# A depthwise convolution of two chunks moved from one diagonal stationary matrix and a vector chain to sixteen 32x32 tiles of the array

## The reference, cut to what matters

```python
def conformer_conv(h, w_pw1, b_pw1, w_dw, b_dw, ln_g, ln_b, w_pw2, b_pw2):
    u = h @ w_pw1 + b_pw1
    a, gate = jnp.split(u, 2, axis=-1)
    u = a * jax.nn.sigmoid(gate)
    u = lax.conv_general_dilated(u, w_dw[:, None, :], window_strides=(1,),
        padding=[(15, 15)], ..., feature_group_count=D_MODEL) + b_dw
    u = jax.nn.silu(layer_norm(u, ln_g, ln_b))
    return u @ w_pw2 + b_pw2
```

## Time and profile before

| | us |
|---|---|
| median of three runs | 2699.52 |
| the profiled execution | 2699.71 |
| its span | 2697.9 |
| TensorE busy | 2617.3 (97%) |
| VectorE busy | 1937.0 (72%) |
| ScalarE busy | 1224.2 (45%) |
| granted TensorE clock, mean | 0.98 |

### The profile page before, as it was taken

One profiled execution on the slowest core, in us unless ns is written; L12 is line 12 of the kernel. 1 busy time (PEld: TensorE's weight loads), 2 busy tenths in 40 slices (PEclk: granted clock), 3 DMA queues, 4 the chain that ended last, 5 costly groups with the idle time before them and its releaser, 6 DMA issues.

```text
span 2697.9 us, 39482 instructions
## 1 busy us (share of the span) xinstructions
PE 2617.3 (97%) x14741; PEld 2283.7 (85%) x14741; DVE 1937.0 (72%) x2749; ACT 1224.2 (45%) x1595; POOL 101.7 (4%) x145
## 2 busy tenths in 40 slices
PE   5799999999998999999999999998999999999998
PEld 4788888888887888888888888887888888888887
DVE  6987778886888888855666657998676644566554
ACT  2245644444554655544555552004454443444443
POOL 0011111100001000000000000000000000000000
PEclk7699999999999999999999999999999999999999
DMA  9898677765777777755666554552666555666554
GB/s 361 306 299 258 214 249 241 246 202 161 230 255 237 234 246 248 239 186 188 189 190 188 187 164 145 152 154 83 204 181 190 187 188 190 189 190 187 188 187 133
DMA packets 492727, 557.35 MB, mean 207 GB/s; under 512 B 18872, under 2 KB 458425, under 8 KB 492345
## 3 DMA queue, kind: packets, MB, share of 16 engines
q1 hardware_dynamic: 474169, 488.50, 56.4%
q0 software_dynamic: 18432, 67.12, 8.0%
HBM read 553.45 MB, written 2.10 MB: 206 GB/s over the span
## 4 chain that ended last, share of the span: by engine, by line
PE 91%; DVE 5%; DMA 3%; issue 1%; ACT 1%; SPq 0%; POOL 0%; DVEq 0%; ACTq 0%
PE ps L1631 53%; PE ps L1633 26%; PE ps L1961 8%; DMA att<-in_w_ada 2%; DVE wlo L949 1%; DVE tCDE L1072 1%; PE ms L1979 1%; PE ms L1682 0%; DVE att L1072 0%; PE ms L1815 0%; PE ms L1662 0%; DVE norm_rows L1053 0%; PE ms L1705 0%; DVE norm_rows L988 0%; DMA ada<-in_w_ada 0%
## 5 line engine op out<-in xcount | busy, mean ns | idle before, releaser
L949 DVE TENSOR_TENSOR wlo<-raw,whi 128x1024 fp32r<-128x1024 f32 x794 | 971.1, 1224 | 612.8 <-ACT whi L582 603.8
L1631 PE MATMUL ps<-xhl,whi 128*128 128x512 f32 x4352 | 1385.9, 400 | 15.5 <-DVE xhl L1529 6.4
L582 ACT CAST whi<-raw 128x1024 fp32r<-128x1024 f32 x794 | 831.7, 1051 | 1059.7 <-PE ps L1633 1049.2
L1633 PEld LDWEIGHTS ps<-xhl,wlo 128*128 128x128 f32 x4352 | 822.9, 189 | 195.3
L1633 PE MATMUL ps<-xhl,wlo 128*128 128x256 f32 x4352 | 859.5, 279 | 0.0
L1631 PEld LDWEIGHTS ps<-xhl,whi 128*128 128x128 f32 x4352 | 669.1, 190 | 25.6 <-issue 25.3
L1631 PE MATMUL ps<-ghl,whi 128*128 128x512 f32 x1024 | 319.5, 393 | 0.0
L1633 PEld LDWEIGHTS ps<-ghl,wlo 128*128 128x128 f32 x1024 | 192.2, 188 | 44.5
L1961 PE MATMUL ps<-xg,raw 128*128 128x256 f32 x1024 | 221.3, 379 | 0.0
L1631 PE MATMUL ps<-fhl,whi 128*128 128x512 f32 x704 | 219.3, 392 | 0.0
L1961 PEld LDWEIGHTS ps<-xg,raw 128*128 128x128 f32 x1024 | 194.5, 190 | 26.4
(11 more groups left out here) (263 smaller groups left out, 1452.2 us busy)
## 6 DMA issues: line engine op xcount, KB each, us to landing
raw<-in_w_in SPq DMA_DIRECT2D x176, 512.0 KB, 4.4
raw<-in_w_up SPq DMA_DIRECT2D x176, 512.0 KB, 3.9
ada<-in_w_ada POOLq DMA_DIRECT2D x128, 512.0 KB, 4.8
raw<-in_ffn_w_up SPq DMA_DIRECT2D x128, 512.0 KB, 3.8
raw<-in_ffn_w_down SPq DMA_DIRECT2D x128, 512.0 KB, 3.4
raw<-in_conv_w_pw SPq DMA_DIRECT2D x96, 512.0 KB, 3.7
raw<-in_w_down SPq DMA_DIRECT2D x88, 512.0 KB, 3.3
att<-in_w_ada SPq DMA_DIRECT2D x32, 1024.0 KB, 8.7
```

What stands on the lines that cost most here:

```text
L582: nc.scalar.copy(whi[t % SPL][:, :, :], raw[t % RAW][:, :, :]).then_inc(s_hi, 1)
L949: nc.vector.tensor_tensor(wlo[t % SPL][:, :, :], raw[t % RAW][:, :, :], whi[t % SPL][:, :, :].bitcast(F32), ALU.subtract).then_inc(s_lo, 1)
L1631: mm(o[:, m, :, :], whi[t % SPL][:, c, m * P:(m + 1) * P], x, start=first and c == 0, stop=last and c == KC - 1, skip_group_check=True)
L1633: ins = mm(o[:, m, 0, :], wlo[t % SPL][:, c, m * P:(m + 1) * P], x[:, 0, :], start=False, stop=last and c == KC - 1, skip_group_check=True)
```

## The change

Both chunks go to TensorE, which is used as sixteen tiles of 32x32. A tile takes 32 channels (a row strip) and writes 32 PSUM partitions (a column strip). Column strip `lane` takes taps 8*lane to 8*lane+7 (seven for the last), so that a strip of 32 channels is convolved in four partial sums, which lie on the four groups of 32 partitions of one bank; the four row strips have a bank each. A chunk is 31 taps times 4 strips, 124 matmuls with 32x32 stationary and 256 columns, in the order: tap within the lane, lane, strip. The partial sums are copied from PSUM to `lanes`, two strips by ScalarE and two by VectorE, and folded by TensorE: for each strip a 128x32 stationary matrix of four stacked identities adds the four lanes and puts them on the strip's 32 partitions. ScalarE reads the folded chunk out with the bias, and the ones matmul adds it to the mean. The stationary 32x32 diagonals of all taps are made by VectorE with one multiplication a chunk, in place of ScalarE's 31; the constants grow by 32 columns. `taps_alternating` is gone. The mean's sum moves from `bank_o` to a bank of `ps[1]`.

```diff
@@ -78,7 +78,10 @@
 G_DN2 = [169, 193]
-BY_DIAGONAL = 15
+BY_TILES = (14, 15)
+QUAD = 32
+LANES = P // QUAD
+LANE_TAPS = -(-TAPS // LANES)
 COL_KI, COL_GATE = 7168, 7248
@@ -150,7 +153,8 @@
 C_ID, C_SW128, C_SW64, C_TRI, C_PAST, C_NEG, C_FREQ, C_SIGN = 0, 128, 256, 384, 512, 896, 1280, 1282
-NCONST = 1284
+C_FOLD = 1284
+NCONST = C_FOLD + QUAD
@@ -158,6 +162,7 @@
     c[i, C_ID + i] = 1
+    c[i, C_FOLD + i % QUAD] = 1
     c[i, C_SW128 + (i + 64) % 128] = 1
@@ -257,9 +262,9 @@
         pg = sb("pg", [P, PC, T], F32, conv)
-        odd = sb("odd", [P, T], F32, conv)
+        lanes = sb("lanes", [P, 2, LANES, T], F32, conv)
         by_pairs = sb("by_pairs", [P, 2, T], F32, conv)
-        diag = sb("diag", [P, TAPS, P], F32, conv)
+        strip_diag = sb("strip_diag", [P, 2, TAPS, QUAD], F32, conv)
         conv.close()
@@ -267,6 +272,8 @@
+        lane_halves = [[ps[a][:, :, 0, :] for a in range(2)], [ms[a][:, 0:3:2, :] for a in range(2)]]
+        sum_mean = ps[1][:, 0, 0, :]
         turned_out = xg[:, 0:DC, :].rearrange("p (h c) t -> p h (c t)", h=2)
@@ -369,8 +376,11 @@
         s_edge = sem("padding_cleared")
-        s_diag = sem("tap_diagonals_made")
-        s_dwt = sem("depthwise_chunk_by_tensor")
+        s_diag = sem("strip_diagonals_made")
+        s_lanes = sem("depthwise_lanes_by_tensor")
+        s_lanesa = sem("depthwise_lanes_copied_by_scalar")
+        s_lanesv = sem("depthwise_lanes_copied_by_vector")
+        s_dwt = sem("depthwise_lanes_added")
         s_dwtc = sem("depthwise_chunk_copied")
@@ -824,9 +834,6 @@
             act.wait_ge(s_used, SPL + T_PW1)
-            for tap in range(TAPS):
-                ins = nc.scalar.activation(diag[:, tap, :], ident, ACT.Copy, scale=col("conv_w_dw_2", DC * tap + BY_DIAGONAL))
-            ins.then_inc(s_diag, 1)
             act.wait_ge(s_free[(G_PW1 + 1) % 2], free_at(G_PW1 + 1))
@@ -841,8 +848,12 @@
                 split_hi(0, T_PW2 + q)
-            act.wait_ge(s_dwt, 1)
-            nc.scalar.activation(ucv[:, BY_DIAGONAL, :], ms[0][:, 0, :], ACT.Identity, bias=col("conv_b_dw_2", BY_DIAGONAL)).then_inc(s_dwtc, 1)
+            for k in range(2):
+                act.wait_ge(s_lanes, k + 1)
+                nc.scalar.copy(lanes[:, k, 0:2, :], lane_halves[k][0]).then_inc(s_lanesa, 1)
+            for k, c in enumerate(BY_TILES):
+                act.wait_ge(s_dwt, k + 1)
+                nc.scalar.activation(ucv[:, c, :], ps[0][:, k, 0, :], ACT.Identity, bias=col("conv_b_dw_2", c)).then_inc(s_dwtc, 1)
@@ -1446,23 +1457,6 @@
-            def taps_alternating(c, before):
-
-                for tap in range(TAPS):
-                    src = upad[:, c, tap:tap + T]
-                    w = col("conv_w_dw_2", DC * tap + c)
-                    dst = odd[:, :] if tap % 2 else ucv[:, c, :]
-                    if tap == 0:
-                        dve.wait_ge(s_u, c + 1)
-                        nc.vector.tensor_scalar(dst, src, w, col("conv_b_dw_2", c), ALU.mult, ALU.add).then_inc(s_dwd, 1)
-                    elif tap == 1:
-                        nc.vector.tensor_scalar(dst, src, w, None, ALU.mult).then_inc(s_dwd, 1)
-                    else:
-                        dve.wait_ge(s_dwd, before + tap - 1)
-                        nc.vector.scalar_tensor_tensor(dst, src, w, dst, ALU.mult, ALU.add).then_inc(s_dwd, 1)
-                dve.wait_ge(s_dwd, before + TAPS)
-                nc.vector.tensor_tensor(ucv[:, c, :], ucv[:, c, :], odd[:, :], ALU.add).then_inc(s_dwd, 1)
-
@@ -1497,6 +1491,10 @@
             dve.wait_ge(s_used, SPL + T_PW1)
+            by_tap = cols[:, AT["conv_w_dw_2"]:AT["conv_w_dw_2"] + DC * TAPS].rearrange("p (t c) -> p t c", c=DC)
+            for k, c in enumerate(BY_TILES):
+                nc.vector.tensor_tensor(strip_diag[:, k, :, :], cons[:, C_FOLD:C_FOLD + QUAD].unsqueeze(1).to_broadcast([P, TAPS, QUAD]),
+                                        by_tap[:, :, c:c + 1].to_broadcast([P, TAPS, QUAD]), ALU.mult).then_inc(s_diag, 1)
             rooted(pa, G_PW1, T_PW1 + 4)
@@ -1504,10 +1502,12 @@
                 add_pair(s - 1)
-            taps_alternating(14, 7 * 2 * TAPS)
+            for k in range(2):
+                dve.wait_ge(s_lanes, k + 1)
+                nc.vector.tensor_copy(lanes[:, k, 2:4, :], lane_halves[k][1]).then_inc(s_lanesv, 1)
...
             dve.wait_ge(s_mean, 1)
-            sv.did(nc.vector.tensor_scalar(nwt[:, :], bank_o[:, 0:T], 1.0 / D, None, ALU.mult))
+            sv.did(nc.vector.tensor_scalar(nwt[:, :], sum_mean, 1.0 / D, None, ALU.mult))
             sv.wait()
@@ -1974,16 +1974,34 @@
             pe.wait_ge(s_edge, 2)
-            pe.wait_ge(s_diag, 1)
-            for tap in range(TAPS):
-                ins = mm(ms[0][:, 0, :], diag[:, tap, :], upad[:, BY_DIAGONAL, tap:tap + T], start=tap == 0, stop=tap == TAPS - 1)
-            ins.then_inc(s_dwt, 1)
+            pe.wait_ge(s_diag, 2)
+            for k, c in enumerate(BY_TILES):
+                for n in range(LANE_TAPS):
+                    for lane in range(LANES):
+                        tap = LANE_TAPS * lane + n
+                        if tap == TAPS:
+                            continue
+                        for strip in range(LANES):
+                            here = slice(QUAD * strip, QUAD * (strip + 1))
+                            ins = mm(lane_halves[k][strip // 2][QUAD * lane:QUAD * (lane + 1), strip % 2, :], strip_diag[here, k, tap, :], upad[here, c, tap:tap + T],
+                                     start=n == 0, stop=tap in (LANE_TAPS * (lane + 1) - 1, TAPS - 1), skip_group_check=True)
+                ins.then_inc(s_lanes, 1)
+            def lanes_added(k):
+
+                pe.wait_ge(s_lanesa, k + 1)
+                pe.wait_ge(s_lanesv, k + 1)
+                for strip in range(LANES):
+                    ins = mm(ps[0][QUAD * strip:QUAD * (strip + 1), k, 0, :], cons[:, C_FOLD:C_FOLD + QUAD], lanes[:, k, strip, :], start=True, stop=True)
+                ins.then_inc(s_dwt, 1)
+
+            lanes_added(0)
             pe.wait_ge(s_pair, 6)
-            pe.wait_ge(s_dwd, 15 * TAPS + 1)
-            for i, x in enumerate((by_pairs[:, 0, :], by_pairs[:, 1, :], ucv[:, 14, :], ucv[:, 15, :])):
-                if i == 3:
-                    pe.wait_ge(s_dwtc, 1)
-                ins = mm(bank_o[:, 0:T], ones[:, :], x, start=i == 0, stop=i == 3)
+            for m in range(2):
+                mm(sum_mean, ones[:, :], by_pairs[:, m, :], start=m == 0, stop=False, skip_group_check=True)
+            lanes_added(1)
+            for k, c in enumerate(BY_TILES):
+                pe.wait_ge(s_dwtc, k + 1)
+                ins = mm(sum_mean, ones[:, :], ucv[:, c, :], start=False, stop=k == 1, skip_group_check=True)
             ins.then_inc(s_mean, 1)
...
             for j in range(8):
```

## The result

| | before | after |
|---|---|---|
| median of 13 runs each, us | 2700.69 | 2705.61 |
| the profiled execution, us | 2699.71 | 2702.47 |
| its span, us | 2697.9 | 2700.6 |
| first tile or diagonal product starts, us | 1840.93 | 1842.97 |
| from there to the mean read by VectorE, us | 15.42 | 15.47 |

The ratio is 1.0018, with a 95% interval of 1.0010 to 1.0025: 4.9 us slower. The table already tells where to look. The stretch that the change rewrites takes as long as before. Most of the loss stands ahead of it: of the 2.7 us between the two profiled executions, 2.04 are a late start of the first tile, 0.05 lie in the stretch, and 0.6 lie behind it, where nothing was changed; their cause is open.

A forecast was written before the change was run, and what follows sets the result against it. The kernel was taken as a chain of matmuls, TensorE busy 97%. Tiles 13.3 + fold 1.07 + pair sums 0.86 + fold 1.07 + read-out 0.68 + ones 0.60 = 17.6 us against 15.42, 2.2 slower: 2701.7, range 2694.5 to 2719.

The forecast's parts named there:

- 16 KB more of constants at the start: nothing.: Loading the wider constants at the start of the program was claimed to cost nothing.
- Sixteen tiles, 13.3 us: Tile matmuls of both chunks on TensorE: four row strips at a time, products in order within a strip, 13.3 us.
- The port: Tile weight loads: if one goes at a time through a common port, 27 ns each, 496 take 13.4 us.
- rival A: Faster: column strips overlap as well, tiles take 6.9 us, total 2695.3, or 2694.0 with folds all at once; chance 0.19.
- rival B: Slower: instruction supply limits the tiles at 58 ns a load and matmul, 28.8 us, total 2717.2; chance 0.22.
- The folds: TensorE's adding of a chunk's lanes behind the tiles: 1.07 us each, 0.43 all at once, 1.72 in series.
- The pair sums: TensorE adds the two pair sums for the mean after the first fold: 0.86 us.
- read-out and ones: After chunk 15's fold: matmul end and ScalarE's read-out 0.68 us, then the ones matmul 0.60 us.
- The hidden parts: Small diagonals (2.4 us) and lane copies were claimed hidden beside other work; nothing was given for dropping ScalarE's 31 diagonals.
- C: Slower: lanes of one strip don't overlap, tiles 26.7 us and folds 1.72 each, total 2716.4; chance 0.14.
- D: The change doesn't do what it says: tiles run in series, 106.6 us, total near 2796; chance 0.04.
- first case: Tile phase with all sixteen tiles running at once: 3.4 us a chunk, 6.9 us for both.

The follow-up runs named there:

- e1: The changed kernel with constants as narrow as before, VectorE adding up the fold matrix from four identity blocks: 2700.88 us, ratio 1.0000.
- e2: The kernel before with only its constants 32 columns wider: 2704.86 us, ratio 1.0017.
- e5: The kernel before with the constants' tile 32 columns wider in SBUF alone, nothing more loaded: 2704.12 us, ratio 1.0013.
- e0: The changed kernel measured once more, unaltered: 2704.91 us, ratio 1.0019.
- e3: The changed kernel with 128 instead of 256 columns in all tile products but the first of each lane: 2704.14 us in one execution.
- e10: e7 with the landing tiles also begun at multiples of 512 bytes: 2696.51 us, ratio 0.9989.
- e11: e10 a second time: 2697.80 us, ratio 0.9989.
- e7: e1 with chunk 14 shared, TensorE making taps 0 to 11 and VectorE taps 12 to 30: 2699.63 us, ratio 0.9997.
- e12: e7 a second time: 2699.40 us, ratio 0.9994.

## Why the prediction came near by the wrong sum

The range (2694.5 to 2719) held, and the forecast that the change loses a little came true. The number, 2701.7, was 3.9 us low, and the forecast's own range of 2698 to 2705 was missed by 0.6. The reason failed. Forecast was +2.2 us, all from the stretch; found is 4.9 us, with +0.05 in the stretch and e1, e2 and e5 show 3 to 5 us of it to come from the start of the program. One error of 2.1 us upward in the stretch stood against one of 3 to 5 us downward at the start, so that the sum came near is luck. By its own steps:

- **"16 KB more of constants at the start: nothing."** This is the step that failed. It was right on the bytes (the wider load landed in 4.5 us where 4.2 were) and didn't ask what lies behind the constants in SBUF. Their 128 bytes a partition moved the landing tile of the first modulation off a multiple of 512 bytes. The loads there are waited for, the rate fell from 402 to 381 GB/s, and five waits grew by 3.6 us. e1 takes this away and has 4.7 us less than after (2700.88 against 2705.61, and 4.0 less than e0); e5 puts it alone into the kernel before, 3.1 us.
- **Sixteen tiles, 13.3 us: 11.9 measured.** The mechanism was wrong with the size. Forecast were row strips side by side with the lanes in order, and weight loads in turns; the records show sixteen tiles at once and thirty loads within 0.1 us. The port was no limit: the stream's 19.4 ns a pair (14.3 in e3) is under its 27. The column strips overlap, which was rival A's case, but A's 6.9 us aren't reached: a stream at hand takes 19.4 ns a matmul, 9.6 us for 496, where A's columns would be 13.9 ns each. The rest of the 11.9 us is the two pauses, where the starts stand 0.89 and 1.12 us apart, and the last matmul's own time. The pauses fit rival B's mechanism, the supply of instructions, though at 27 to 32 ns a pair over the second half and not 58 over all. (B's bound is a little off too: 32 ns a pair would lose 4.6 us, and the 5.4 us of 0.2% begin at 33 ns.)
- **The folds, 1.07 us each: 0.57.** They ran nearly all at once (the forecast's lower end was 0.43). **The pair sums**, 0.86 forecast, 1.11; **read-out and ones**, 1.28 forecast, 1.33. So 13.3 + 1.07 + 0.86 + 1.07 + 1.28 = 17.6 stands against 11.9 + 0.57 + 1.11 + 0.57 + 1.33 = 15.5.
- **The hidden parts**, the small diagonals, the copies and ScalarE's 31 diagonals, were hidden. The granted clock stayed at 1.00 in the tiles, and the first piece of the next product moved with the mean, by 2.08 and 2.09 us.
- **Rival A** would have decided below 11.1 us of tiles; measured 11.9. **C** and **D** are out by the records of the first 0.1 us.

The Trainium skill, "TensorE: Matmul & The Clock Gate", Part 3, says that a pack of sixteen such tiles runs 10.6 times as fast as in series, each starting some 4 ns after the last. In the trace the sixteen matmuls of the first pack do start within 0.11 us, but some 7.5 ns apart, not 4. In this stream of 31 packs each matmul takes 19.4 ns while instructions are at hand, where the series needs 215: 11 times, near the page's factor. Over all 496, with the pauses, it is 11.9 us where 106.6 would be the series, 9.0 times. The prediction took this rule for the 6.9 us of its first case. By the page's factor it is 106.6 / 10.6 = 10.1 us, an estimate, and much nearer to the 9.6 us of 496 matmuls at 19.4 ns. Part 1 of the same page states about 62 ns a MATMUL for a sequencer that decodes by its own code. No run here shows that: from one batch's start to the next the slowest took 32 ns a pair.

## What to carry to other kernels

When a change makes a tile in on-chip memory wider, look at which tiles lie behind it, above all those into which waited-for transfers land: here 128 bytes cost 3 to 5 us, more than the tiles gave, and making the small matrix on the chip instead cost nothing that could be told (e1). When a profile shows the same time in the stretch that was changed, go back to the first place where the two chains of waits part. And packing small matmuls multiplies instructions: count them. Beyond the first 251 pairs of weight load and matmul the stream here stood still every 128 pairs, and by the reading above it waited for instructions. An engine idle beside it is then worth giving a share of the work: the stretch became 4 us shorter, and the whole 2.7 to 4.1 us in e10 and e11, though only 1.1 to 1.4, within the noise, in e7 and e12.

## What the runs showed of the hardware that was not expected

- Loads of 1024 KB into a tile that begins 64 or 128 bytes past a multiple of 512 moved 380 to 382 GB/s with the DMA engines full, 401 to 403 at a multiple. It is the destination in SBUF that counts here; a wider row in HBM changed nothing (401). Other offsets were not tried.
- A stream of 32x32 float32 weight loads and matmuls pauses first after 251 pairs and then after each 128 pairs, 256 instructions, for 0.3 to 1.9 us. Fewer columns make the batches shorter (2.10 us for 2.74) and the pauses longer, at 3.5 to 4.0 us from batch to batch.
- Where instructions are at hand, a 32x32 tile's matmul of 256 columns adds 19.4 ns to the stream, and with 128 columns in most of them 14.3 ns. Why half the columns don't give half the time there is open.
